# Constants loaded inside the stages that use them, first weights split in parts, in a two-layer decoder step

## The reference, cut to what matters

```python
# layer 0: rmsnorm, one input projection, mLSTM heads (4) and gated DeltaNet heads (4), output projection
hm = mlstm_chunked(q, k, v, mi + b_i, log_sigmoid(mf + b_f), c0, n0, m0)
hm = rmsnorm(hm, mi_norm) * sigmoid(mo)            # the gates of the stage "mlstm"
og = rmsnorm(gated_delta_chunked(...), gd_norm) * silu(gz)
x = x + concat(hm, og) @ w_out_even
x = x + relu(rmsnorm(x, norm_mlp) @ w_up) ** 2 @ w_down
# layer 1: rmsnorm, one input projection, NSA heads (8) and FoX heads (8), output projection, MLP
def compress(kf, pos_emb, w1, w2):                 # blocks of 32 tokens, stride 16
    c = kf.reshape(B, Tp // 16, 16, G, D)
    blocks = concat([c[:, :-1], c[:, 1:]], axis=2) + pos_emb
    return silu(blocks.reshape(B, nc, G, 32 * D) @ w1) @ w2
y = rmsnorm(x, norm_final)
```

## Time and profile before

| what | us |
|---|---|
| median of 3 runs (3794.78 to 3803.72) | 3797.23 |
| the profiled execution: its time | 3796.18 |
| the profiled execution: span from first to last instruction | 3794.4 |
| PE busy | 3455.1 (91% of the span) |
| PE weight loads busy (beside the matmuls) | 3194.5 (84%) |
| DVE busy | 1353.7 (36%) |
| POOL busy | 1204.5 (32%) |
| ACT busy | 606.9 (16%) |
| mean granted PE clock | 0.926 of full |

### The profile page before, as it was taken

How to read it: one execution, slowest core, us unless ns; L and a number is a source line. 1 busy time by engine, 2 the same in 40 slices (tenths; PEclk the granted TensorE clock), 3 DMA queues, 4 the chain that set the end, 5 groups by cost and what they waited for, 6 DMA issues and landing times. The chain is left out here.

```text
span 3794.4 us, 47463 instructions
## 1 busy us (share of the span) xinstructions
PE 3455.1 (91%) x20367; PEld 3194.5 (84%) x20367; DVE 1353.7 (36%) x1914; ACT 606.9 (16%) x1117; POOL 1204.5 (32%) x588
## 2 busy tenths in 40 slices
PE   6989887999999999979898797899778999999998
PEld 6989767889999999978694386788557999999998
DVE  4941145434323231430011254555324332323242
ACT  4310133221000000110001032233122100000012
POOL 4433212533444444425130121111103344444442
PEclk8999877899999999989997898899868999999999
DMA  4111222221111111122122213000122111111111
GB/s 127 45 34 52 83 23 44 66 98 35 45 45 45 45 45 45 57 106 92 55 71 64 64 35 71 7 7 7 56 84 91 35 45 45 45 45 45 43 45 60
DMA packets 302887, 204.11 MB, mean 54 GB/s; under 512 B 61985, under 2 KB 283507, under 8 KB 302136
## 3 DMA queue, kind: packets, MB, share of 16 engines
q1 hardware_dynamic: 297184, 200.65, 18.8%
q10 hardware_dynamic: 5496, 0.45, 0.1%
HBM read 158.87 MB, written 33.40 MB: 51 GB/s over the span
## 5 line engine op out<-in xcount | busy, mean ns | idle before, releaser
L236 PE MATMUL ps<-u_r,wslots_r 128*128 128x364 f32 x4608 | 772.3, 330 | 0.0
L236 PEld LDWEIGHTS ps<-u_r,wslots_r 128*128 128x128 f32 x4608 | 770.8, 189 | 0.0
L203 POOL TENSOR_TENSOR wslots_r<-rawm,sb_ones 128x1024 fp32r<-128x1024 f32 x133 | 320.7, 2411 | 910.9 <-PE ps L236 873.9
L236 PE MATMUL ps<-hn_r,wslots_r 128*128 128x364 f32 x2880 | 589.7, 331 | 13.2 <-POOLq L197 13.2
L236 PE MATMUL ps<-low_r,wslots_r 128*128 128x364 f32 x2688 | 543.8, 330 | 15.9 <-POOLq L197 15.0
L236 PEld LDWEIGHTS ps<-hn_r,wslots_r 128*128 128x128 f32 x2880 | 497.1, 189 | 13.6 <-POOLq L197 13.6
L236 PEld LDWEIGHTS ps<-low_r,wslots_r 128*128 128x128 f32 x2688 | 462.2, 189 | 16.5 <-POOLq L197 15.3
L205 POOL TENSOR_TENSOR wslots_r<-rawm,wslots_r 128x1024 fp32r<-128x1024 f32 x133 | 380.0, 2857 | 10.4
L1878 DVE TENSOR_TENSOR xT<-xT,ps 128x1092 f32<-128x1092 f32 x80 | 103.3, 1292 | 650.4 <-PE ps L236 632.8
L1600 PE MATMUL ps<-hn_r,wslots_r 128*128 128x364 f32 x1392 | 279.4, 334 | 17.5 <-POOLq L1570 8.9
L1600 PEld LDWEIGHTS ps<-hn_r,wslots_r 128*128 128x128 f32 x1392 | 241.0, 191 | 24.0 <-DVE Z L1830 10.0
(11 more groups left out here) (607 smaller groups left out, 4782.4 us busy)
## 6 DMA issues: line engine op xcount, KB each, us to landing
rawm<-in_w_down SPq DMA_DIRECT2D x64, 512.0 KB, 3.6
rawm<-in_w_up SPq DMA_DIRECT2D x63, 512.0 KB, 4.0
raw<-in_w_in_even SPq DMA_DIRECT2D x28, 512.0 KB, 3.7
xT<-x_saved SPq DMA_DIRECT2D x2, 4368.0 KB
xT<-in_cache_fox_kv SPq DMA_DIRECT2D x16, 512.0 KB, 3.7
more_r<-more_r SPq DMA_DIRECT2D x28, 256.0 KB
panel_raw<-in_w_in_odd SPq DMA_DIRECT2D x6, 1024.0 KB, 5.4
x_saved<-Z SPq DMA_DIRECT2D x1, 4368.0 KB
```

The costliest lines, as they stand in the source:

```text
L203: nc.gpsimd.tensor_tensor(r32(half[0][:, g % 2]), raw[:, g % 2], one, ALU.mult).then_inc(s["high"], 1)
L236: mm = pe.matmul(view[n % 2][:, c, :], r32(half[a][:, n % 2, k, :]), r32(t["x"][b][:, k, CH * c:CH * (c + 1)]), start=(k == 0 and (a, b) = ...
```

## The change

- The stages const, const0, const1 and const2 are gone, `load_constants` too. Their DMAs are issued in loadx, mlstm, tokmajor and sample, each with a semaphore on which the first user waits. The gains come as 40 contiguous rows in three DMAs, and PE transposes them.
- In mlstm SP issues sel and the masks first, level and block32 behind the gates. PE does the column transposes ahead of the products with sel. The gates of all slots come in one DMA; POOL multiplies them in four operations, one for each head. The factors are taken in three batches (slots 0 to 4, 5 and 6, 7 and 8), and the turned-back slots follow `finished`.
- A stream with `first=True` loads its first tile in two halves, which ACT and DVE split; POOL begins with the second tile. tokmajor's panel 0 comes in four parts of 512 KB.
- In tables `X[kv]` is 128 x 8 x 386: element a of all slots side by side. The position embeddings come in two DMAs for each kv instead of one.

```diff
-            if first:
-                first_load(sp, s, W, tiles)
+            if first:
+                for x in (0, 1):
+                    sp.dma_start(raw[:, 0, 4 * x:4 * x + 4], weight_rows(tiles[0])[:, 4 * x:4 * x + 4]).then_inc(s[f"raw{x}"], 16)
...
+                if g == 2 and first:
+                    need(sp, "dve", ("first_low", 1))
...
-            if first:
-                first_split(nc, pool, s, W)
             pool.sem_inc(s["split"], 1)
...
+                    if first and n == 0 and k % 4 == 0:
+                        need(pe, "dve", ("first_low", k // 4))
...
+            def first_high(x):
+                if first:
+                    act.wait_ge(s[f"raw{x}"], 16)
+                    nc.scalar.activation(r32(half[0][:, 0, 4 * x:4 * x + 4]), raw[:, 0, 4 * x:4 * x + 4], ACT.Copy) \
+                        .then_inc(act_.sem, act_.mark(("first_high", x)))
+            if not halves:
+                first_high(0)
+                first_high(1)
...
             for k, (x, hi, lo) in enumerate(halves):
                 nc.scalar.activation(r32(hi), x, ACT.Copy).then_inc(act_.sem, act_.mark(("half_high", k)))
+                if k in (1, 2):
+                    first_high(k - 1)
...
+            def first_low(x):
+                if first:
+                    need(dve, "act", ("first_high", x))
+                    V.tensor_tensor(r32(half[1][:, 0, 4 * x:4 * x + 4]), raw[:, 0, 4 * x:4 * x + 4], r32(half[0][:, 0, 4 * x:4 * x + 4]), ALU.subtract) \
+                        .then_inc(dve_.sem, dve_.mark(("first_low", x)))
...
# load_x
+                    if i == 0:
+                        sp.dma_start(ident[:], I["c_ident"]).then_inc(s["ident"], 16)
+                        for n, g in enumerate(("norm_mix", "norm_mlp")):
+                            sp.dma_start(gains[16 * n:16 * n + 16], I[g].rearrange("l (k p) -> (l k) p", p=P)).then_inc(s["gains"], 16)
+                        sp.dma_start(gains[32:40], I["norm_final"].rearrange("(k p) -> k p", p=P)).then_inc(s["gains"], 16)
+                    if i == 1:
+                        sp.dma_start(C["ones"][:], I["c_ones"]).then_inc(s["ones"], 16)
...
+                    if i == 0:
+                        pe.wait_ge(s["gains"], 48)
+                        pe.transpose(bank(ps, 7)[:, 0:40], gains, ident[0:40, 0:40]).then_inc(pe_.sem, pe_.mark("gains"))
...
# mlstm
+    batches = (slice(0, 5), slice(5, 7), slice(7, 9))
+    finished = {4: (0, 1), 5: (2, 3), 6: (4,), 7: (5, 6)}
...
+            sp.dma_start(C["sel"][:], I["c_sel"]).then_inc(s["sel"], 16)
+            for n in ("maskS", "maskP"):
+                sp.dma_start(C[n][:], I["c_" + n]).then_inc(s["masks"], 16)
...
+            sp.dma_start(gate, G[0:4].rearrange("h p t -> p h t")).then_inc(s["gate"], 16)
...
+            pool.wait_ge(s["gate"], 16)
+            for h in hs4:
+                step(("gate", h), E.tensor_tensor(gate[:, h], gate[:, h], gam[:, h:h + 1].broadcast_to([P, TP]), ALU.mult))
...
+                for k in finished.get(i, ()):
+                    gated(k)
+                    if k < 3:
+                        scaled(k + 2)
+                if i == 5:
+                    factors(1)
+                if i == 6:
+                    scaled(5)
+                    scaled(6)
+            factors(2)
+            scaled(7)
+            scaled(8)
+            for k in (7, 8):
                 gated(k)
...
# token_major
-            for x in (0, 1):
-                panel_load(sp, s[f"first{x}"], panel, 0, x)
+            for q in range(4):
+                rows = panel["w"][256 * q:256 * (q + 1), PANELS[0][0]:PANELS[0][0] + 512].rearrange("(k p) m -> p k m", p=P)
+                sp.dma_start(panel["raw"][:, q // 2, 2 * (q % 2):2 * (q % 2) + 2, :], rows).then_inc(s[f"first{q}"], 16)
...
# tables
-    X = [arena([P, 8 * (UNITS + 2)]) for _ in range(2)]
+    X = [arena([P, 8, UNITS + 2]) for _ in range(2)]
...
-                    c0 = 8 * (a // 8) + a % 8
-                    mm = pe.matmul(hb, w1[:, kv, a, P * m:P * (m + 1)], X[kv][:, c0:c0 + 8 * UNITS + 1:8], start=(a == 0), stop=(a == 15))
+                    mm = pe.matmul(hb, w1[:, kv, a, P * m:P * (m + 1)], X[kv][:, a % 8, a // 8:a // 8 + UNITS + 1], start=(a == 0), stop=(a == 15))
...
-                    src = bank(ps, u % 2)[:, 256 * kv:256 * kv + 256].rearrange("p (g n) -> p g n", g=2)
+                    src = bank(ps, u % 2)[:, 256 * kv:256 * kv + 256].rearrange("p (g n a) -> p g n a", g=2, a=8)
+                    n0 = 16 * u if u < 4 else 128 + 32 * (u - 4)
+                    to = X[kv][:, :, 0:128] if u < 4 else X[kv][:, :, n0:n0 + 32]
+                    dst = to.rearrange("p a (g n) -> p g n a", g=2)
```

More of the change, by code:

```diff
@@ L153, in stream @@
     raw, half, one = W["raw"], W["half"], W["ones"][:].unsqueeze(1).to_broadcast([P, KT, P])
-    with pr.stage(name, steps=["pe", "act", "dve"], sems=["w0", "w1", "high", "split", "arrive", "leave", "stored"] + (FIRST if following or first else [])) as (block, s):
+    with pr.stage(name, steps=["pe", "act", "dve"], sems=["w0", "w1", "high", "split", "arrive", "leave", "stored", "raw0", "raw1"] + (FIRST if following else [])) as (block, s):
         pe_, act_, dve_ = s["pe"], s["act"], s["dve"]
@@ L484, in spread @@
         return v.rearrange("p (h o) -> p h o", o=1).broadcast_to([v.shape[0], 4, n])
-    with pr.stage("mlstm", steps=["pe", "act", "dve", "pool"], sems=["state", "blocks", "gam", "gate0", "gate1", "st"]) as (block, s):
+    with pr.stage("mlstm", steps=["pe", "act", "dve", "pool"], sems=["sel", "masks", "later", "state", "blocks", "gam", "gate", "st"]) as (block, s):
         pe_, act_, dve_, pool_ = s["pe"], s["act"], s["dve"], s["pool"]
@@ L680, in root @@
                 need(dve_, ("mean", n))
-                step(("root", n), A.activation(part[:, 5 * n:5 * n + 5 - n], part[:, 5 * n:5 * n + 5 - n], ACT.Sqrt))
+                step(("root", n), A.activation(part[:, batches[n]], part[:, batches[n]], ACT.Sqrt))
             def high(k):
@@ L695, in _ @@
                     root(0)
[L696 to L701 removed]
+                if i == 5:
+                    root(1)
+                for k in finished.get(i, ()):
+                    high(k)
+            root(2)
+            for k in (7, 8):
                 high(k)
@@ L2028, in token_major @@
     with pr.stage("tokmajor", steps=["pe", "act", "dve"],
-                  sems=["w0", "w1", "first0", "first1", "halves", "gs", "hist"] + [f"out{k}" for k in range(NSL)]) as (block, s):
+                  sems=["w0", "w1", "first0", "first1", "first2", "first3", "halves", "gs", "hist", "rowvalid", "pages"] + [f"out{k}" for k in range(NSL)]) as (block, s):
         pe_, act_, dve_ = s["pe"], s["act"], s["dve"]
@@ L2089, in _ @@
             sp.wait_ge(s["hist"], 16)
+            sp.wait_ge(s["pages"], 16)
             for k in range(NSL):
@@ L3277, in sample_attention @@
     nmx, rs, cf = arena([NS, 4]), arena([NS, 4]), arena([NS, 4])
-    with pr.stage("sample", steps=["pe", "act", "dve", "pool"], sems=["in0", "in1", "in2", "new", "same"]) as (block, s):
+    with pr.stage("sample", steps=["pe", "act", "dve", "pool"], sems=["in0", "in1", "in2", "new", "same", "mask"]) as (block, s):
         pe_, act_, dve_, pool_ = s["pe"], s["act"], s["dve"], s["pool"]
```

170 lines of the change are left out of this document (67 added, 103 removed).

## The result

The changed kernel takes 3704.45 us (median of 4 runs, 3699.78 to 3706.73), the kernel before on the same chip 3796.01 (4 runs). The profiled execution took 3704.17, with a span of 3702.4.

A forecast was written before the change was run, and what follows sets the result against it. PE, busy 91% of the span, was taken to bound the kernel, with waits at stage starts and slow tables matmuls. Terms summed to 87.5 us off 3796.2, giving 3708.7, as a median 3709.7, so 3710; range 3693 to 3728.

The forecast's parts named there:

- Tables: In tables, L2336's matmuls on adjacent columns take 0.333 us instead of 0.693; net 43.4 us gained, slower ACT copies mostly hidden.
- Start: At kernel start, x loads 7.35 us earlier, but waiting for the gains lengthens ACT's and DVE's chain by 0.9; 6.4 gained.
- const0: Before mlstm's first read-out: the stage's 7.92 us go, sel and two masks cost 1.3; read-out 6.6 earlier, states landing last.
- Gates and batches: Late mlstm: all four DVE waits for gates, 15.5 us, go; with three batches of factors 13.7 gained, bounds 8 and 19.
- two slots of some 0.95 each: mlstm's tail: two slots turned inside the loop instead shorten the tail by some 0.95 us each (L844's 0.69 and handover).
- two read-outs save 2.4 each: mlstm, upper bound only: if shorter idle keeps the clock high, two read-outs of 32 instructions save 2.4 us each.
- First weights: tokmajor, queries, wout1: loading and splitting in parts gains 3.3, 4.0, 4.2 us; wout1 includes some 2 us PE stall at slice 3.
- Strided writes: Rival in tables: ACT's copies into X double and PE waits for all of them; total 3720, chance 10%.
- Square roots: Rival in mlstm: the batch at chunk 5 stalls the loop by 6 us; 3.5 gained instead of 13.7, total 3720, chance 12%.
- The stride not being it: Rival in tables: the 0.693 us comes from something that stays; 43.9 us are missing, total 3754, chance 8%.
- the parts not doing it: Rival at first weights: DMAs in parts land as late as the whole, DVE eats the rest; 11.5 us missing, 3721, 6%.
- Slower by a low clock: Rival: dense products after shortened starts stay at 1.2 GHz; beyond 87 us of them the kernel is slower, chance 2%.

The follow-up runs named there:

- experiment 2: The kernel before with one edit: in tables the elements of all slots lie side by side (position embeddings in four DMAs); 3752.29 us, ratio 0.9885.
- experiment 6: The changed kernel, but tables' slot elements lie in groups, read in steps of 16 bytes (values) and 8 bytes (keys); 3726.76 us, ratio 0.9812.
- experiment 11: The changed kernel, but sel, masks, level and block32 are loaded in a stage of their own ahead of mlstm again; 3708.91 us, ratio 0.9764.
- experiment 5: The changed kernel with mlstm's gates slot by slot and two batches of factors again, constants still loaded inside the stage; 3720.82 us, ratio 0.9804.
- experiment 4: The changed kernel with the factors in two batches again and the old order of turned-back slots, gates still at once; 3704.69 us, ratio 0.9762.
- experiment 1: The changed kernel once more, nothing edited, with profiles compared stage by stage; 3703.09 us, ratio 0.975.
- experiment 7: The changed kernel with first weights as before: queries and wout1 load whole tiles that POOL splits, tokmajor's panel in two parts; 3717.85 us, ratio 0.9798.

## Why the prediction was right, and where a step of it was not

- **Tables, 43.4 predicted, 44.4 measured.** The step "a contiguous column costs 0.865 ns" is the mechanism, and experiment 2 shows it alone. It was mis-sized by little: 0.324 us a matmul, not 0.333. ACT's copies took 0.66, between my bounds, and hid as argued: PE waited 1.3 us for the last in place of 0.9. Whether the new layout must cost this, or only the order in which the copies write it, was not tried (experiment 6).
- **Start, 6.4 against 6.6.** The step "this lengthens the chain by 0.9" was too large: the first scaling starts 6.82 earlier, of 7.35, so the copies of the gains cost it 0.5.
- **const0, 6.6 predicted, 5.5 to 8.1 measured.** At the first read-out the term is nearly right: it comes 6.9 earlier (24.6 to 17.7). The wait was right too, though with less room: in four of the changed kernel's six profiles the last state still ends it. The preparation, which I had put 1.9 ahead of the states, ends 1.1 ahead of them or less, and in two profiles about with them: this is the step of the term that was too short. What the stage kept of the 6.9 depends on the pair of profiles that is compared, 8.1 by experiment 11 and 5.5 by experiment 5.
- **Gates and batches, 13.7 predicted, 13.8 to 16.4 measured.** 13.8 is 145.9 - 132.1, by experiment 11; 16.4 is 140.4 - 124.0, by experiment 5. By my terms gates alone were 15.5 and the three batches cost 1.8; measured are 16.8 and nothing (experiments 4, 5). The failed step is "two slots of some 0.95 each": a slot in the tail is 1.96. Both parts were too low, so that 13.7 lies at the lower edge; that it was nearly met by one of the two measures is luck. The predicted tail of 9.3 from the last batch's start came out at 9.4 (550.12 to 559.55).
- **mlstm as a whole, 20.3 predicted, 24.1 in this pair of profiles.** Before's mlstm was 139.5 here and 136.4 in experiment 2; with const0's 7.9 that is 145.9 in the mean, against 124.0: 21.9. The other 2 us of the 24.1 are chance. Of the 21.9, 2.4 are the clock, and they are no chance: chunk 6's read-out takes 5.8 to 5.9 us, at 1.2 GHz, in before and in experiments 2 and 5, and 3.4, at 2.4 GHz, in all eleven others. The sum had put this at nothing and kept it for the range's low end ("two read-outs save 2.4 each"); one of the two came true each time. They are part of the 13.8 and of the 16.4 as well.

```profile
552.40:559.00 6.60, 6.60 (x26) 4.68 (x24) 2.33 (x5) 0.81 (x3) 1.43 (x2) 0.50 0.00 0
```
```profile
533.00:537.20 4.20, 4.20 (x31) 2.93 (x29) 1.52 (x4) 2.88 (x7) 1.71 (x2) 1.00 0.00 0
```

- **First weights, 3.3, 4.0, 4.2 against 3.6, 4.1, 5.2.** wout1's step that failed is "PE then stalls some 2 us at slice 3": the stall was 0.57. POOL's two operations on tile 1 fell beside one slice and one half of the first weights; a single slice's low half is slow in its row:

```profile
L328 DVE TENSOR_TENSOR hn_r<-hn,low_r x8: 1281/1286/3499, 2787.3 to 2802.1; 128x1092 fp32r<-128x1092 f32 x8
```

- **Not in the sum at all: the clock in delta.** It took 3.0 us back in this pair, 2.9 in the mean, against mlstm's surplus of 3.8; the total owes part of its nearness to this. By experiment 1's comparison it is probably a cost of the change that the prediction left out. What is left of the 4.5 by which 92.0 exceeds 87.5 is 1.0 each in tables and wout1, 0.9 in mlp1 and writey, which no edit explains, and small change.
- **The rivals.** Strided writes: they did cost more (0.66), and were hidden. Square roots: the batch with its second slot costs the loop about 4 (3.6 in the first pair), which the shorter tail gives back. The stride not being it, and the parts not doing it, are refuted by experiments 2 and 7. Slower by a low clock did not come: the span's mean clock went from 0.926 to 0.930.

## What to carry to other kernels

When a matmul takes the same time at both clocks, look at the step of its moving operand: in these runs a float32 operand needed two elements out of every 16 bytes, not four, and a layout that costs the writing engine more is cheap where that engine waits. When a chain at a stage's end is priced, count every engine in the loop, not the one that waited. Before a term of 2 us is believed from one pair of profiles, compare what the unedited stages do between two profiles of the same kernel.

## What the runs showed of the hardware that was not expected

- The step's cost fits a maximum, not a sum: 0.324, 0.339, 0.678 and 0.692 us for 385 float32 columns at steps of 4, 8, 16 and 32 bytes.
- ACT's copy of 128 x 256 float32 from PSUM into SBUF takes 0.38 us when it writes runs of 256 bytes or more, even if it reads in runs of 8 bytes, and 0.66 when it writes single elements 1544 bytes apart.
- The same instructions take 376 to 384 us in nsa and 199 to 204 in delta; what differs in the windows above is PE's busy time and the granted clock.
- Matmuls of ones for 3.75 us just ahead did not raise the clock for the products behind them: it rose 9.6 to 9.7 us after the barrier of queries with and without them. What would raise it earlier was not tried.
